# Condition products of two hybrid blocks: from TensorE matmuls to multiply-adds on VectorE in lots of four

## The chip, the cores and the metric

The kernel runs on one core of one Trainium2 chip. The metric is the time of one execution in microseconds (us) of device time; a version's time is the median of its runs. A profiled execution gives the span of its instructions and their trace. The engines are called TensorE (PE in the rows; PEld is its weight load), VectorE (DVE), ScalarE (ACT), GpSimd (POOL) and SyncE (SP). ACTq and SPq are the rows of instructions that issue DMAs.

## The reference

A block of two layers (dilated attention, then a state space layer) is followed by a block of two hybrid layers. All is float32, 1024 tokens by 1024 channels. What matters here is the modulation of the hybrid layers: two condition vectors (one for the tokens, one for the context) are multiplied with `w_mod`, which gives shift, scale and gate.

```python
c_act = jax.nn.silu(c)            # (1, 1024)
cc_act = jax.nn.silu(c_ctx)       # (1024,)
for l in range(2):
    x, xc = hybrid_layer(x, xc, c_act, cc_act, w_mod[l], b_mod[l], ...)

def hybrid_layer(...):            # w_mod[l]: (1024, 3072)
    shift, scale, gate = jnp.split(c_act @ w_mod + b_mod, 3, axis=-1)
    h = x * (1 + scale[:, None]) + shift[:, None]
    mod_c = jnp.split(cc_act @ w_mod[:, :n_mod * D_MODEL] + b_mod[:n_mod * D_MODEL], n_mod)
    hc = xc * (1 + mod_c[1]) + mod_c[0]
    ...
```

So there are two vectors of 1024 by two matrices of 1024x3072. The kernel does this work far ahead of the hybrid layers, while the attention layer runs, and keeps the results in DRAM (`mod_rows`).

## The kernel before

**The attention stage.** It walks over eight pairs of heads (hp 0 to 7) and, in each, over three segments (si 0 to 2), one for each group of the dilated attention. A segment has four unit pairs (p = 4*si to 4*si+3). For each, TensorE computes `scores`, VectorE adds the bias and takes the row minimum (`logits`, line 3747), ScalarE takes exponentials (`probs`), TensorE transposes them (`turn_p`), ScalarE copies them out of PSUM (`take_pt`), TensorE multiplies by v (`outputs`, lines 3003 and 3010, and at p % 4 == 3 a transposition of the statistics, line 3015), and VectorE evacuates (`evacuate`, lines 3762 to 3771). Between these steps TensorE computes the projections of the next pair of heads in three passes of split float32 (`proj`, line 2936): 24 matmuls of 512 columns for each half of 512 tokens. `seg_at` says how many are done ahead of each step. The order on every engine is written out by hand, and the engines meet in semaphores. A segment's last `outputs` comes at the start of the next segment, behind 12 projection matmuls.

The last segment (hp 7, si 2) has no projections. A projection half needs its PSUM bank free, that is the evacuation of the half two before it by ScalarE (`evac`, line 1226); behind every second half ScalarE rounds a slot of weights (line 3265) and GpSimd computes its rest (line 2766; for the next stage's weights lines 2757 and 2760).

**The merge.** In a pair's first segment VectorE also merges the three groups of the pair before (`merge_all`). The group weights go out to DRAM (`put_weights`, ScalarE at i == 2) and come back spread over 64 partitions (`spread_weights`, four loads of ScalarE's queue at i == 3, lines 3315 and 3318). VectorE waits for them at i == 4 (part 1, line 3815) and goes on at i == 5 (parts 2 and 0, lines 3818 and 3820). Here i runs from 0 to 7 in `segment_act` and `segment_dve`, two steps to a unit pair: at an even i come `logits` of the next pair and `evacuate` of the one before.

**The condition products.** The 2 x 3072 columns are cut into 12 visits of 512 columns, n = 3*(hp-4)+si, one in each segment of the head pairs 4 to 7. ScalarE loads the weights of visit n in the segment before, at i == 5, in two halves of 256 columns (1 MB each, line 1252). In segment n TensorE computes 12 projection matmuls, the last `outputs` of the segment before, eight more projection matmuls, waits for VectorE's evacuation and then does `mod_mul` (line 1268): 8 blocks of 128 rows by 4 blocks of 128 columns, each with a stationary operand of 32 columns, of which two hold the conditions and 30 are zero (`c_wide`). The four column blocks write four different groups of 32 PSUM partitions. VectorE adds the bias in `mod_add` (line 1278), and TensorE waits for that at the segment's first `outputs`.

Of the kernel before, what the change touches and what calls it, by code (L numbers as in the profile page):

```python
# [16 lines left out]
ALU = mybir.AluOpType  # L17
# [4 lines left out]
P = 128  # L22
# [115 lines left out]
def build(nc, io, out):  # L138
    x_in = io["x"].rearrange("b s d -> (b s) d")
    ctx = ExitStack()  # L140
    with ctx:
# [1092 lines left out]
        c_wide = region(29712, KT, 32)  # L1234
# [4 lines left out]
        m_wide, m_c, m_mul, m_sum, m_stored = [sem(n) for n in ("m_wide", "m_c", "m_mul", "m_sum", "m_stored")]  # L1239
# [7 lines left out]
        def load_mod_w(act, n):  # L1247
# [3 lines left out]
            for i in range(2):  # L1251
                act.dma_start(MOD_W[i], w[:, :, c0 + CTX * i:c0 + CTX * (i + 1)]).then_inc(m_w, 16)
# [8 lines left out]

        def mod_mul(pe, n):

            pe.wait_ge(m_wide, 2)
            pe.wait_ge(m_w, 32 * (n + 1))
            for k in range(KT):
                for c in range(4):
                    ins = nc.tensor.matmul(psum[32 * c:32 * c + 32, 6, 0:P], c_wide[:, k, :],
                                           MOD_W[c // 2][:, k, P * (c % 2):P * (c % 2) + P],
                                           start=(k == 0), stop=(k == KT - 1))  # L1270
            ins.then_inc(m_mul, 1)

        def mod_add(dve, n):
# [4 lines left out]
            nc.vector.tensor_tensor(MOD_ROWS[:, n], MOD_ROWS[:, n], psum[:, 6, 0:P], ALU.add).then_inc(m_sum, 1)  # L1278
# [1631 lines left out]
        def _(pe):  # L2910
# [78 lines left out]
            def outputs(hp, p):  # L2989
# [7 lines left out]
                if p % 4 == 0 and mod_of(hp, si) is not None:  # L2997
                    pe.wait_ge(m_sum, mod_of(hp, si) + 1)
# [50 lines left out]
            def segment(hp, si, par, prev, with_proj):  # L3049
# [175 lines left out]
        def _(act):  # L3225
# [168 lines left out]
            def segment_act(hp, si, par, prev, with_proj, more):  # L3394
# [17 lines left out]
                for i in range(8):  # L3412
# [196 lines left out]
        def _(dve):  # L3609
# [141 lines left out]
            def evacuate(hp, p, par):  # L3751
# [3 lines left out]
                if p % 4 == 3:  # L3755
# [6 lines left out]
                    nc.vector.tensor_copy(dst, src).then_inc(st_rows, 1)  # L3762
# [253 lines left out]
```

## Time and profile before

| | us |
|---|---|
| median of 3 runs (lowest to highest) | 3149.55 (3145.45 to 3152.84) |
| profiled execution, its own time | 3148.35 |
| its span, first to last instruction | 3146.5 |
| TensorE busy | 3056.2 (97%) |
| VectorE busy | 1497.5 (48%) |
| ScalarE busy | 1229.6 (39%) |
| GpSimd busy | 808.1 (26%) |

The busy time of an engine is the time in which at least one of its instructions runs; TensorE's matmuls overlap, so the mean of one (0.39 us for 512 columns) is longer than its pitch (0.23 us). The share is a mean over stages. The mean granted clock of TensorE is 0.993 of full speed. Times in the rows are counted from the start of the span. In a timeline each row gives the start, the duration, engine, line, operation and operands, how many such instructions are merged into it, and in brackets how long the engine had been idle and what ended it.

### The profile page before, as it was taken

To read this page: it belongs to the slowest core of one execution; us is meant where nothing else is said; L and a number is where in the kernel's file an instruction comes from. 1 tells how busy PE (TensorE), PEld (TensorE's weight loads), DVE (VectorE), ACT (ScalarE), POOL (GpSimd) and SP (SyncE) were. 2 spreads that over 40 slices of the span, in tenths; PEclk is the share of its full clock that TensorE was granted. 3 is DMA by queue.
4 is the path that set the end of the run, shared out by engine and by line. 5 is a ranking of instruction groups with operands and counts; after the bars stand their busy time and mean duration, and the time that the engine had idled before them with its cause. 6 is when DMAs were issued, how large, how long until landed. Compare 5 with 4: busy or idle time off the path is not lost.

```text
span 3146.5 us, 54425 instructions
## 1 busy us (share of the span) xinstructions
PE 3056.2 (97%) x22219; PEld 2474.9 (79%) x22219; DVE 1497.5 (48%) x3462; ACT 1229.6 (39%) x2590; POOL 808.1 (26%) x407
## 2 busy tenths in 40 slices
PE   7999999999999998999999999999999999999999
PEld 5877778788787786777888888877788788877777
DVE  3343232332313235659632535665556845565676
ACT  4443434444433434513321523345333333344342
POOL 2155565111112114133254111110223111111231
PEclk9999999999999999999999999999999999999999
DMA  6113223144423333423454311111003332111113
GB/s 198 46 49 88 74 74 88 54 130 119 121 92 91 98 86 103 138 71 107 146 189 144 109 41 41 39 28 32 25 28 112 114 79 54 33 34 33 36 47 141
DMA packets 327792, 262.22 MB, mean 83 GB/s; under 512 B 78123, under 2 KB 291659, under 8 KB 327548
## 3 DMA queue, kind: packets, MB, share of 16 engines
q1 hardware_dynamic: 187692, 131.09, 14.5%
q10 hardware_dynamic: 139856, 127.69, 13.6%
q8 instruction: 176, 2.88, 0.4%
q14 instruction: 68, 0.56, 0.1%
HBM read 215.50 MB, written 45.97 MB: 83 GB/s over the span
## 4 chain that ended last, share of the span: by engine, by line
PE 51%; DVE 5%; ACT 3%; issue 2%; DMA 1%; ACTq 0%; POOL 0%; DVEq 0%; POOLq 0%
PE psum L1550 24%; PE psum L387 10%; PE psum L312 5%; PE psum L1686 2%; PE psum L1666 2%; PE psum L1675 1%; DVE act_lo L2582 1%; PE psum L1590 1%; PE psum L1579 1%; PE psum L3177 1%; PE psum L1596 1%; PE psum L3186 0%; PE psum L3157 0%; PE psum L1623 0%; DVE arena L2344 0%
## 5 line engine op out<-in xcount | busy, mean ns | idle before, releaser
L2766 POOL TENSOR_TENSOR w_lo<-w_raw,w_hi 128x1024 fp32r<-128x1024 f32 x122 | 300.7, 2465 | 1434.8 <-ACT w_hi L3265 743.4
L1550 PE MATMUL psum<-act_hi,w_hi 128*128 128x512 f32 (+1 forms) x1376 | 513.5, 373 | 12.0 <-ACT arena L1779 6.3
L2936 PE MATMUL psum<-act_hi,w_hi 128*128 128x512 f32 x1280 | 505.1, 395 | 6.3 <-ACT arena L1226 5.4
L2936 PE MATMUL psum<-act_lo,w_hi 128*128 128x512 f32 x1280 | 507.4, 396 | 0.0
L2936 PE MATMUL psum<-act_hi,w_lo 128*128 128x512 f32 x1280 | 505.1, 395 | 0.0
L1550 PE MATMUL psum<-act_lo,w_hi 128*128 128x512 f32 (+1 forms) x1376 | 504.5, 367 | 0.0
L1550 PE MATMUL psum<-act_hi,w_lo 128*128 128x512 f32 (+1 forms) x1376 | 503.9, 366 | 0.0
L3747 DVE CUSTOM_DVE_ANT_0 arena<-psum,arena 128x256 f32<-128x256 f32 (+2 forms) x384 | 103.4, 325 | 445.5 <-PE psum L2985 178.0
L1550 PEld LDWEIGHTS psum<-act_hi,w_hi 128*128 128x128 f32 x1376 | 260.4, 189 | 68.4 <-issue 17.9
L1550 PEld LDWEIGHTS psum<-act_hi,w_lo 128*128 128x128 f32 x1376 | 260.7, 189 | 45.6 <-issue 5.5
L1550 PEld LDWEIGHTS psum<-act_lo,w_hi 128*128 128x128 f32 x1376 | 260.9, 190 | 43.9 <-issue 7.6
L2936 PEld LDWEIGHTS psum<-act_hi,w_hi 128*128 128x128 f32 x1280 | 241.6, 189 | 60.1 <-ACT arena L1226 6.4
L2936 PEld LDWEIGHTS psum<-act_lo,w_hi 128*128 128x128 f32 x1280 | 241.0, 188 | 58.9 <-issue 9.8
L2936 PEld LDWEIGHTS psum<-act_hi,w_lo 128*128 128x128 f32 x1280 | 240.7, 188 | 56.9 <-issue 8.3
L2757 POOL TENSOR_TENSOR w_hi<-w_raw,one 128x1024 fp32r<-128x1024 f32 x48 | 96.7, 2014 | 657.5 <-PE psum L1550 274.6
L1226 ACT ACTIVATE arena<-psum 128x512 f32<-128x512 f32 x144 | 133.3, 926 | 188.7 <-PE psum L2936 151.9
L3274 ACT ACTIVATE arena<-arena 128x256 f32<-128x256 f32 (+2 forms) x384 | 161.6, 423 | 73.3 <-DVE arena L3747 73.0
L1779 ACT ACTIVATE arena<-psum 128x512 f32<-128x512 f32 (+1 forms) x102 | 70.7, 694 | 200.3 <-PE psum L1550 197.5
L3329 ACT COPY arena<-psum 128x1024 f32<-128x1024 f32 x64 | 64.9, 1015 | 173.0 <-PE psum L3010 145.7
L2760 POOL TENSOR_TENSOR w_lo<-w_raw,w_hi 128x1024 fp32r<-128x1024 f32 x48 | 124.0, 2584 | 3.8
L1875 ACT COPY arena<-psum 128x640 f32<-128x640 f32 (+1 forms) x108 | 71.3, 660 | 128.6 <-PE psum L1686 97.9
L1866 ACT ACTIVATE arena<-arena 128x384 f32<-128x384 f32 (+1 forms) x96 | 56.8, 592 | 150.1 <-DVE arena L2106 150.1
(409 smaller groups left out, 5355.7 us busy)
## 6 DMA issues: line engine op xcount, KB each, us to landing
w_raw<-in_attn_w_in SPq DMA_DIRECT2D x80, 512.0 KB, 3.8
w_raw<-in_w_in SPq DMA_DIRECT2D x64, 512.0 KB, 3.9
spare<-in_w_mod ACTq DMA_DIRECT2D x24, 1024.0 KB, 8.4
x<-arena ACTq DMA_DIRECT2D x24, 512.0 KB, 2.9
arena<-weight_rows ACTq DMA_DIRECT2D x16, 512.0 KB
w_raw<-in_ssm_w_in SPq DMA_DIRECT2D x16, 512.0 KB, 3.7
arena<-mc_mat ACTq DMA_DIRECT2D x16, 512.0 KB, 4.1
arena<-x ACTq DMA_DIRECT2D x16, 512.0 KB, 5.4
```

Source lines behind the costliest of these rows:

```text
L312: ins = nc.tensor.matmul(psum[:, t, :], a[:, k, t * P:(t + 1) * P], w[:, par, i * 512:(i + 1) * 512], start=(k == 0 and a is act_hi and w ...
L387: ins = nc.tensor.matmul(psum[:, bank + c, :], a[:, k, t * P:(t + 1) * P], w[:, c * 512:(c + 1) * 512], start=(i == 0 and w is hi and a is ...
L1226: return nc.scalar.activation(dst, src, ACT.Copy, scale=SCALE if p % 3 == 0 else 1.0)
L1550: ins = nc.tensor.matmul(psum[:, n % 2, 0:c], w[:, slot % 2, k * P:(k + 1) * P], a[:, k, c0:c0 + c], start=(m == 0), stop=(m == 23))
L1779: C.activation(dst, src, ACT.Copy, scale=SCALE if (j < 3 and q == 0) or (j >= 3 and q == 1) else 1.0).then_inc(g_evac[n % 2], 1)
L1875: C.copy(PT2[h][:, c0:N_LOG], flat(6, 2)[:, c0:N_LOG]).then_inc(u_pt, 1)
L2757: G.tensor_tensor(w_hi[:, par], w_raw[:, par], one[:, 0:1].to_broadcast([P, 1024]), ALU.mult).then_inc(slot_hi, 1)
L2760: G.tensor_tensor(w_lo[:, par], w_raw[:, par], w_hi[:, par].bitcast(F32), ALU.subtract).then_inc(slot_split, 1)
L2766: G.tensor_tensor(w_lo[:, par], w_raw[:, par], w_hi[:, par].bitcast(F32), ALU.subtract).then_inc(slot_split, 1)
L2936: ins = nc.tensor.matmul(psum[:, h % 2, :], w[:, (3 + j) % 2, k * P:(k + 1) * P], a[:, k, c:c + 512], start=(m == 0), stop=(m == 23))
L3274: nc.scalar.activation(lg, lg, ACT.Exp, scale=-1.0, bias=st[:, 2 + h, u:u + 1], accum_out=st[:, h, u:u + 1]).then_inc(u_probs, 1)
L3747: nc.vector.tensor_tensor_reduce(LOG[:, a, logit_cols(g, u, h)], logit_psum(g, u, a, h), BIAS[:, h, bias_cols(g, u)], -1.0, 3e38, ALU.add, ...
```

## The change

The products move to VectorE. For each block of 128 rows (k) and each condition (i), one operation multiplies a 128x256 tile of weights with a scalar for each partition (the condition's value for that row) and adds it to a sum `MOD_SUM` of 128 partitions. A half of 256 columns takes 16 operations, a visit 32. They are done in lots of four, one after each step i of the segment before (`next_mod`), lots 0 to 3 for the first half of the columns, 4 to 7 for the second; visit 0 is done in four lots of eight at i = 4 to 7. TensorE then only adds up the 128 partitions: `mod_mul` has 8 matmuls in place of 32, with a stationary operand that has a column of ones, and stands at the start of the segment's last `outputs`. It waits for all 32 operations. `mod_add` follows inside `evacuate`.

The loads are issued by halves: the second half of a visit at i == 2 (behind lot 0), the first half of the visit after it at i == 5 (behind lot 4); for visit 0 both at i == 3. The eight projection matmuls that stood ahead of the product, its wait for the evacuation and the wait of `outputs` for `mod_add` go.

```diff
+        def mod_part(dve, n, half, k0, k1):
+            dve.wait_ge(m_w, 32 * n + (32 if n == 0 else 16 * (half + 1)))
+            if n == 0 and k0 == 0:
+                dve.wait_ge(m_c, 33)
+                dve.wait_ge(k_put, CHUNK_PUT * N_CHUNKS)
+            if n > 0:
+                dve.wait_ge(m_mul, n)
+            for k in range(k0, k1):
+                for i in range(2):
+                    w, total = MOD_W[half][:, k, :], MOD_SUM[:, i, CTX * half:CTX * half + CTX]
+                    c = c_cols[:, k, i:i + 1]
+                    if k == 0:
+                        nc.vector.tensor_scalar(total, w, c, None, ALU.mult).then_inc(m_part, 1)
+                    else:
+                        dve.wait_ge(m_part, 32 * n + 16 * half + 2 * k + i - 1)
+                        nc.vector.scalar_tensor_tensor(total, w, c, total, ALU.mult, ALU.add).then_inc(m_part, 1)
         def mod_mul(pe, n):
-            pe.wait_ge(m_wide, 2)
-            pe.wait_ge(m_w, 32 * (n + 1))
-            for k in range(KT):
+            if n == 0:
+                pe.wait_ge(n_pad, 3)
+            pe.wait_ge(m_part, 32 * (n + 1))
+            if n > 0:
+                pe.wait_ge(m_sum, n)
+            for i in range(2):
                 for c in range(4):
-                    ins = nc.tensor.matmul(psum[32 * c:32 * c + 32, 6, 0:P], c_wide[:, k, :],
-                                           MOD_W[c // 2][:, k, P * (c % 2):P * (c % 2) + P],
-                                           start=(k == 0), stop=(k == KT - 1))
+                    ins = nc.tensor.matmul(psum[32 * c:32 * c + 32, 6, 384:512], MOD_ONE[:, i, :],
+                                           MOD_SUM[:, i, P * c:P * c + P], start=(i == 0), stop=(i == 1))
             ins.then_inc(m_mul, 1)
@@ outputs
-                if p % 4 == 0 and mod_of(hp, si) is not None:
-                    pe.wait_ge(m_sum, mod_of(hp, si) + 1)
+                if p % 4 == 3 and next_mod(hp, si) is not None:
+                    mod_mul(pe, next_mod(hp, si))
@@ segment
-                if mod_of(hp, si) is not None:
-                    if with_proj:
-                        proj(hp, h0, at, at + 8)
-                        at += 8
-                    pe.wait_ge(u_evac, NU * hp + 8 * si)
-                    mod_mul(pe, mod_of(hp, si))
@@ segment_act
-                    if i == 5 and -1 <= m < N_MOD - 1:
-                        if m >= 0:
-                            act.wait_ge(m_mul, m + 1)
-                        load_mod_w(act, m + 1)
+                    if i == 2 and 0 <= m < N_MOD - 1:
+                        act.wait_ge(m_part, 32 * (m + 1) + 4)
+                        load_mod_w(act, m + 1, 1)
+                    if i == (7 if m == -1 else 5) and -1 <= m < N_MOD - 2:
+                        act.wait_ge(m_part, 32 * (m + 1) + 20)
+                        load_mod_w(act, m + 2, 0)
                     if i == 3 and m == -1:
                         act.wait_ge(k_put, CHUNK_PUT * N_CHUNKS)
                         act.wait_ge(k_cst, 32 * N_CHUNKS)
+                        for half in range(2):
+                            load_mod_w(act, 0, half)
                         load_mod_bias(act)
@@ evacuate, between the copy of the statistics and that of the outputs
+                    if next_mod(hp, p // 4) is not None:
+                        mod_add(dve, next_mod(hp, p // 4))
@@ segment_dve, after the merge parts of step i
+                    if next_mod(hp, si) == 0 and i >= 4:
+                        mod_part(dve, 0, i // 6, 4 * (i % 2), 4 * (i % 2) + 4)
+                    if next_mod(hp, si) is not None and next_mod(hp, si) > 0:
+                        mod_part(dve, next_mod(hp, si), i // 4, 2 * (i % 4), 2 * (i % 4) + 2)
```

## Rows read from the trace of the kernel before

**Rows 1.** Busy time of each engine in the stretch of the products.

```profile
core 0: us, PE busy (x) PEld busy (x) DVE busy (x) ACT busy (x) POOL busy (x), PEclk, DMA share, GB/s
655.00:1197.00 542.00, 538.72 (x4625) 430.86 (x4618) 144.02 (x571) 216.41 (x524) 97.12 (x41) 1.00 0.36 105
```

**Rows 2.** Groups of instructions, shapes apart; busy us, mean ns, idle before.

```profile
L1268 PE MATMUL psum<-spare,arena 128*32 128x128 f32 x768 | 23.5, 274 | 1.2 <-DVE arena L3771 1.2
```

**Rows 3.** Timeline of TensorE around the first product.

```profile
662.13 0.39 PE L2936 MATMUL psum<-act_lo,w_hi 128*128 128x512 f32 x1
662.45 1.95 PE L1268 MATMUL psum<-spare,arena 128*32 128x128 f32 x64
664.33 1.09 PE L2967 MATMUL psum<-ident,arena 128*128 128x128 f32 x8
```

**Rows 4.** Groups of VectorE at the end of the kernel, shapes apart.

```profile
L2505 DVE SCALAR_TENSOR_TENSOR arena<-arena 128x512 f32<-128x512 f32 x2 | 1.4, 750 | 0.0
```

**Rows 5.** Timeline of VectorE, the same two operations.

```profile
3142.61 1.42 DVE L2505 SCALAR_TENSOR_TENSOR arena<-arena 128x512 f32<-128x512 f32 x2
```

**Rows 6.** Timeline, TensorE and VectorE at the end of segment 4/1.

```profile
752.22 0.89 PE L3010 MATMUL psum<-arena 64*64 64x128 f32 x24
756.93 0.89 PE L3010 MATMUL psum<-arena 64*64 64x128 f32 x24
...
753.71 0.42 DVE L3771 TENSOR_TENSOR arena<-arena,psum 128x256 f32<-128x256 f32 x1
```

**Rows 7.** Timeline, VectorE and TensorE at the end of segment 4/0.

```profile
693.76 1.99 DVE L3815 TENSOR_TENSOR arena<-arena 128x1024 f32<-128x1024 f32 x1 [4.16 <-DMA arena<-weight_rows]
...
698.81 0.47 DVE L3767 COPY arena<-psum 128x256 f32<-128x256 f32 x1
...
700.64 0.46 PE L3003 MATMUL psum<-arena 64*64 64x64 f32 x16
```

**Rows 8.** The same places at the end of segment 7/0.

```profile
1132.85 2.00 DVE L3815 TENSOR_TENSOR arena<-arena 128x1024 f32<-128x1024 f32 x1 [5.20 <-DMA arena<-weight_rows]
...
1138.68 0.46 PE L3003 MATMUL psum<-arena 64*64 64x64 f32 x16
```

**Rows 9.** Timeline at the end of segment 3/2: VectorE, GpSimd, TensorE.

```profile
656.11 0.42 DVE L3771 TENSOR_TENSOR arena<-arena,psum 128x256 f32<-128x256 f32 x1
...
658.69 2.38 POOL L2766 TENSOR_TENSOR w_lo<-w_raw,w_hi 128x1024 fp32r<-128x1024 f32 x1 [13.68 <-ACT w_hi L3265]
...
659.30 1.10 PE L3010 MATMUL psum<-arena 64*64 64x128 f32 x32
```

**Rows 10.** Timeline of segment 6/0: GpSimd and VectorE.

```profile
985.07 4.81 POOL L2766 TENSOR_TENSOR w_lo<-w_raw,w_hi 128x1024 fp32r<-128x1024 f32 x1 [14.29 <-ACT w_hi L3265]
...
987.53 4.23 DVE L3820 TENSOR_TENSOR arena<-arena 128x1024 f32<-128x1024 f32 x1
```

**Rows 11.** Timeline of ScalarE's queue in segment 4/0.

```profile
684.11 0.58 ACTq L3315 DMA_DIRECT2D arena<-weight_rows  x1
```

**Rows 12.** Stretch after 694 us: columns as in Rows 1.

```profile
694.00:699.00 5.00, 5.00 (x38) 3.94 (x38) 5.00 (x4) 1.36 (x3) 0.00 (x0) 1.00 1.10 375
```

**Rows 13.** Timeline at the end of segment 5/1: GpSimd, TensorE.

```profile
901.15 2.39 POOL L2766 TENSOR_TENSOR w_lo<-w_raw,w_hi 128x1024 fp32r<-128x1024 f32 x1 [12.54 <-ACT w_hi L3265]
...
902.18 0.89 PE L3010 MATMUL psum<-arena 64*64 64x128 f32 x24
```

**Rows 14.** Timeline at the start of segment 7/2: TensorE, GpSimd.

```profile
1192.36 0.89 PE L3010 MATMUL psum<-arena 64*64 64x128 f32 x24
...
1196.64 1.09 PE L2967 MATMUL psum<-ident,arena 128*128 128x128 f32 x8
...
1192.44 1.90 POOL L2757 TENSOR_TENSOR w_hi<-w_raw,one 128x1024 fp32r<-128x1024 f32 x1 [10.54 <-PE psum L2936]
1194.41 2.39 POOL L2760 TENSOR_TENSOR w_lo<-w_raw,w_hi 128x1024 fp32r<-128x1024 f32 x1
```

**Rows 15.** Stretches around a pause of TensorE in a hybrid layer.

```profile
2204.00:2206.00 2.00, 0.17 (x1) 0.17 (x2) 1.50 (x7) 2.00 (x8) 0.00 (x0) 0.96 0.00 0
2206.00:2208.00 2.00, 2.00 (x25) 1.67 (x29) 0.88 (x3) 0.33 (x2) 0.00 (x0) 0.50 0.21 25
```

More of the change, by code:

```diff
@@ L1231, in build @@
         halves = lambda g2: slice(64 * g2, 64 * g2 + 64)
-        c_wide = region(29712, KT, 32)
+        MOD_SUM = region(29168, 2, 512)
+        MOD_ONE = region(26128, 2, 32)
         N_MOD = 12
@@ L1238, in build @@
         mod_rows = dram("mod_rows", (2, 2, 3072))
-        m_wide, m_c, m_mul, m_sum, m_stored = [sem(n) for n in ("m_wide", "m_c", "m_mul", "m_sum", "m_stored")]
+        m_part, m_c, m_mul, m_sum, m_stored = [sem(n) for n in ("m_part", "m_c", "m_mul", "m_sum", "m_stored")]
         m_bias, m_w = sem("m_bias"), sem("m_w")
@@ L1245, in mod_of, with next_mod, load_mod_w @@
             return n if 0 <= n < N_MOD else None
-        def load_mod_w(act, n):
+        def next_mod(hp, si):
+            n = 3 * (hp - 4) + si + 1
+            return n if 0 <= n < N_MOD else None
+        def load_mod_w(act, n, half):
             l, c0 = n // 6, 512 * (n % 6)
             w = io["w_mod_2"][l].rearrange("(k p) c -> p k c", p=P)
-            for i in range(2):
-                act.dma_start(MOD_W[i], w[:, :, c0 + CTX * i:c0 + CTX * (i + 1)]).then_inc(m_w, 16)
+            act.dma_start(MOD_W[half], w[:, :, c0 + CTX * half:c0 + CTX * (half + 1)]).then_inc(m_w, 16)
         def load_mod_bias(act):
@@ L1277, in mod_add @@
             dve.wait_ge(m_mul, n + 1)
-            nc.vector.tensor_tensor(MOD_ROWS[:, n], MOD_ROWS[:, n], psum[:, 6, 0:P], ALU.add).then_inc(m_sum, 1)
+            nc.vector.tensor_tensor(MOD_ROWS[:, n], MOD_ROWS[:, n], psum[:, 6, 384:512], ALU.add).then_inc(m_sum, 1)
         def store_mod(act, l):
@@ L3852, in segment_dve @@
                     merge_all(hp - 1, 1 - par, "three")
-                if mod_of(hp, si) is not None:
-                    mod_add(dve, mod_of(hp, si))
                 dve.wait_ge(v_turned, 6 * hp + (2 * si + 2))
@@ L3880, in segment_dve @@
                         nc.vector.memset(PAD[0:31, :, :], 0.0).then_inc(n_pad, 1)
-                        nc.vector.memset(c_wide[:, :, :], 0.0).then_inc(m_wide, 1)
-                        dve.wait_ge(m_wide, 1)
-                        nc.vector.tensor_copy(c_wide[:, :, 0:2], c_cols[:, :, :]).then_inc(m_wide, 1)
+                        nc.vector.memset(MOD_ONE[:, :, :], 0.0).then_inc(n_pad, 1)
+                        dve.wait_ge(n_pad, 2)
+                        nc.vector.memset(MOD_ONE.rearrange("p a b -> p (a b)")[:, 0:64:33], 1.0).then_inc(n_pad, 1)
                     if hp == 0 and si == 2 and i < 4:
                         k_squares(1 << i)
+                    if next_mod(hp, si) == 0 and i >= 4:
+                        mod_part(dve, 0, i // 6, 4 * (i % 2), 4 * (i % 2) + 4)
+                    if next_mod(hp, si) is not None and next_mod(hp, si) > 0:
+                        mod_part(dve, next_mod(hp, si), i // 4, 2 * (i % 4), 2 * (i % 4) + 2)
                     if si == 1 and i == 4:
```

## The prediction

> **What bounds the kernel now.** I began with the busy times of each engine over the stretch in which the condition products run, from 655 to 1197 us [rows 1]. The reader is to see TensorE (PE) busy for 538.7 of 542 us at the full clock, VectorE (DVE) for only 144 us. So here TensorE sets the time: what it is spared is won, and a wait that it gets is lost, microsecond for microsecond. VectorE has 398 us to spare, but it works in order, and what counts is what it has between two waits of TensorE. So I then read the timeline at the places where the new waits stand: the end of each of the three segments of a head pair, where `outputs` of the segment's last unit pair now begins with `mod_mul`.
>
> **What is removed from TensorE.** The 384 products (two records each) have 23.5 us busy [rows 2]. One visit: the last projection matmul before it starts at 662.13, its slot is 0.23, and the next work starts at 664.33 [rows 3], so a product costs 664.33 - 662.36 = 1.97 us. Eight matmuls of the same form in place of 32 cost 8/32 of 1.88 = 0.47. The gain is 1.50 us for each visit; the last visit stands in a segment with no projections and is counted by itself below, so 11 x 1.50 = **-16.5 us**. The eight projection matmuls that stood ahead of the product are not lost or saved: they move behind the scores, and everything after that in the segment moves with them by 1.8 us.
>
> **What is added to VectorE.** 12 x 32 operations of 128x256, nearly all scalar_tensor_tensor with a scalar per partition. Rows have this form at 128x512: 750 ns each [rows 4], two in a row in 1.42 us [rows 5], so the second starts 0.67 after the first, which is 512 elements at 0.96 per ns (0.533) plus 0.137. For 256 that gives 0.267 + 0.137 = 0.40 us. A lot of four is 1.6 us, 12 x 8 lots are 155 us. The waits inside a lot are on the operation two before, ended by then. In the middle of a segment this is hidden behind the projections: the unit pairs there are 8 to 12 us apart and a pair brings some 2.3 us of VectorE work plus two lots, 3.2. It costs 0 there; without that cover it would be the whole 3.2.
>
> **Where it is not hidden.** `mod_mul` waits for lot 7, and lots 6 and 7 come after the evacuation of the third unit pair. In a middle segment TensorE starts these outputs at 752.22 and comes to the last outputs at 756.93; the second evacuating operation starts at 753.71 [rows 6], leaves VectorE free 0.34 later, and eight operations plus 0.13 for the end and the release give 753.71 + 0.34 + 3.23 + 0.13 = 757.41. That is 0.5 us late. The third segments come to the same 0.5. For the six such ends (products 2, 3, 5, 6, 8, 9): 3.0 us.
>
> In the first segment of a pair VectorE merges the groups of the pair before. It waits for the weight rows until 693.76, and the evacuation starts at 698.81 only; TensorE is at the last outputs at 700.64 [rows 7]. Now lots 4 to 7 all stand in that chain, since lot 4 is behind the merge that waits: 693.76 + 5.05 + 4 x 1.62 + 0.35 + 0.13 = 705.8, so 5.1 us late. The last such pair has less room, 1132.85 to 1138.68 [rows 8], and 6.3 us by the same sum; the other two give 5.8 and 5.2 (the one at 984 us has a merge of 4.23 in its chain already [rows 10]). Together 22.4 us. ScalarE stands in this too: its load at i == 5 waits for lot 4, so it evacuates a projection half some 7 us later than now, and TensorE stands still for that instead, inside the same lateness. I count it once.
>
> Product 0 is done in lots of eight at i = 4 to 7: from 656.11 + 0.34, 16 x 0.404 + 0.13 gives 663.0 against 659.30 [rows 9], 3.7 us.
>
> **The half load that is moved.** ScalarE issued both halves at i == 5, behind the four loads of the weight rows (i == 3, first at 684.11 [rows 11]). Now one half of 1 MB goes out at i == 2, ahead of them in the same queue. When only these loads are served they move 375 GB/s [rows 12], so 1 MB takes 2.8 us; the queue is idle for some of it (24 KB are written and waited for meanwhile). Bounds 0 and 2.8; I take 1.0, since the issue comes some 1.5 us before 684.11. Four times: 4 us. The other half is issued after lot 4 with most of a segment to land: 0. The bias loads and SP's loads keep their places; one half is issued behind lot 0, so nothing of SP's queue waits for it.
>
> **GpSimd.** At 985.07 GpSimd's split took 4.81 us instead of 2.39, and VectorE's merge at 987.53 took 4.23 where its like took 2.2 [rows 10]: two operations that read SBUF stand in each other's way, and the one that comes second waits for the whole of the other. The lots read two operands from SBUF. A split of 2.4 us starts 1.0 us before the last outputs [rows 13] in five of the six ends above, so inside lots 6 and 7; at 658.69 [rows 9] it lies inside product 0's. In a first segment it lies inside the lengthened chain. The bounds are 0 and 2.4 for each. At 985 the split had let two merges pass before it got its turn, so where only one microsecond of lots is left I take half, 5 x 1.2 = 6.0; where the chain is long, all: 4 x 2.4 = 9.6, and 2.4 for product 0.
> The Trainium skill (SBUF — State Buffer, "SBUF: two separate sides") says that VectorE with two SBUF inputs and GpSimd take one port pair as an exclusive lock for a whole instruction. By that rule each of the five would pay the full 2.4, and the sum below would be 6 us more; the trace shows the lock, but also the split passed over.
>
> **The last visit.** Segment 3 of the last pair has no projections. TensorE is at the last outputs at 1192.36 and at the transposes of v at 1196.64; GpSimd splits at 1192.44 and 1194.41 [rows 14]. The lots start near 1192.1: one operation, the first split, one operation, the second split (to 1197.2), then six in 2.4 us, so 1199.75. Product 0.47, outputs and statistics 1.1: the transposes start at 1201.3, **+4.7 us**, its gain included.
>
> **The clock.** After TensorE had stood idle for 1.8 us at 2204, the granted clock went from full to half for some 3.4 us [rows 15]; matmuls run half as fast there, 1.7 us lost. I charge 1.7 to each wait over 1.9 us: four first segments, product 0, and half of the five: 7.5 x 1.7 = 12.8 us. Bounds: 0, and 2.5 each.
>
> **Sum.** Waits 22.4 + 3.0 + 3.7 = 29.1; loads 4.0; GpSimd 9.6 + 6.0 + 2.4 = 18.0; last visit 4.7; clock 12.8: 68.6. Less 16.5: **+52 us**. The profiled execution took 3148.35, so 3200.5; the median is 1.2 above it: **3202 us**.
>
> **Rivals.** (a) *Such short operations do not meet the splits*, and the short waits do not move the clock. Then the waits are 29.1, the last visit +0.6, gain 16.5: +13, 3163 us. For it: the split passed over at 985. Against: every long pair that met. (b) *Every meeting of a lot with a split costs its whole 2.4 us*, with the load at 2.8 and the clock at its upper bound: +52 + 6 + 7 + 9 = +74, 3224 us. For it: the merge of 4.23. Against: in the short ends only two or three operations are left when the split comes. (That case is the rule of the Trainium skill, SBUF — State Buffer, named above.) (c) *The lots are hidden.* If an operation took 0.27 us or less (twice the rate on the elements), lots 6 and 7 would end before TensorE arrives, and the first segments would have to free 5 us by weight rows that come earlier. Then it is faster by up to 12 x 1.5 = 18 us, 3132 us. It decides once all waits together stay below 16.5 us. Against it: no operation with two SBUF inputs in the rows runs faster than one element per cycle. (d) *Waits and gain cancel*: two first-segment waits of 5 us and a few short ones, 3150 us.
>
> **Chances.** The forecast 0.50, (a) 0.20, (b) 0.13, (c) 0.10, (d) 0.07. This kernel's measurement can tell about 0.2%, 6.3 us, from no change. Range 3156 to 3226: below lies (c), (d), and above little of (b). The likeliest case's own range is 3180 to 3220. Faster 0.10, same 0.07, slower 0.83.
>
> **What the profile would show.** TensorE's busy time for the product a quarter, some 6 us. An idle time ahead of the product ended by VectorE's lots: 0.5 to 3 us at the ends of middle and third segments, 6 to 9 us at first segments, part of it ahead of a projection half, ended by ScalarE's evacuation. VectorE's busy time up by some 170 us; the longest of the new operations near 2.8 us where a split lies under it, the split itself hardly longer. The weight rows' merge starts about 1 us later after the scores of the second unit pair. Clock dips after the waits of the first segments. I am wrong if the operation's pitch is not 0.40 us, if lots 4 and 5 run before the merge's wait ends, or if TensorE reaches the last outputs later than now for another reason, which would make room for the lots.

## The result and the profile after

The changed kernel takes 3212.56 us (median of 4 runs, 3208.60 to 3215.35) against 3149.01 for the kernel before in the same comparison: ratio 1.0201, 95% interval 1.0188 to 1.0213. It is slower, far outside the noise; whether by more or by less than 2% the interval leaves open. The profiled execution took 3208.6 with a span of 3206.8, so 60.3 us more than before's 3146.5. Mean granted clock 0.984 against 0.993.

The same work that lay between 655 and 1197 us [rows 1] now ends near 1258, so the first row is to be laid beside that of before. The second shows the stretch of equal length.

```profile
core 0: us, PE busy (x) PEld busy (x) DVE busy (x) ACT busy (x) POOL busy (x), PEclk, DMA share, GB/s
655.00:1258.00 603.00, 544.40 (x4049) 432.95 (x4047) 311.05 (x949) 215.86 (x525) 103.84 (x42) 0.95 0.33 95
...
655.00:1197.00 542.00, 491.85 (x3668) 391.00 (x3667) 280.81 (x859) 195.48 (x477) 86.98 (x34) 0.95 0.35 99
```

TensorE idles for 603 - 544.4 = 58.6 us, where it idled for 3.3. That is 55 of the 60 us. Its busy time went up by 5.7 although the products got shorter, and the granted clock of the stretch fell from 1.00 to 0.95. Who ended the idle time stands in the waits of TensorE, between 655 and 1260 us (us in total, times, longest):

```profile
PE psum L1294 <- DVE arena L1283: 41.0, 12, 7.0
PE psum L2961 <- ACT arena L1226: 16.2, 4, 5.9
PE psum L2981 <- DVE arena L3770: 1.4, 1, 1.4
```

L1294 is the product and L1283 the new operation. L2961 is a projection (before: L2936) that needs ScalarE's evacuation L1226; that one had in turn waited for a load issue whose semaphore the lots raise. The groups of the whole trace, shapes apart:

```profile
L1283 DVE SCALAR_TENSOR_TENSOR arena<-spare,c_cols,arena 128x256 f32<-128x256 f32 x336 | 167.8, 568 | 0.0
...
L3840 DVE TENSOR_TENSOR arena<-arena 128x1024 f32<-128x1024 f32 x8 | 18.4, 2298 | 50.0 <-DMA arena<-weight_rows 50.0
L1280 DVE TENSOR_SCALAR arena<-spare,c_cols 128x256 f32<-128x256 f32 x48 | 16.5, 387 | 0.9 <-DVE arena L3865 0.9
...
L1294 PE MATMUL psum<-arena 128*32 128x128 f32 x192 | 10.8, 359 | 41.0 <-DVE arena L1283 41.0
```

The products have 10.8 us busy where [rows 2] had 23.5, over half of it at half clock.

**A first segment.** The timeline of segment 4/0, to be laid beside [rows 7] and [rows 11]:

```profile
682.85 0.60 ACTq L3327 DMA_DIRECT2D weight_rows<-arena  x1
...
683.90 0.40 ACTq L1257 DMA_DIRECT2D spare<-in_w_mod  x1
684.10 3.24 DVE L1283 SCALAR_TENSOR_TENSOR arena<-spare,c_cols,arena 128x256 f32<-128x256 f32 x8
...
687.11 0.59 ACTq L3334 DMA_DIRECT2D arena<-weight_rows  x1
...
699.64 1.98 DVE L3840 TENSOR_TENSOR arena<-arena 128x1024 f32<-128x1024 f32 x1 [7.80 <-DMA arena<-weight_rows]
...
703.42 1.06 ACT L1226 ACTIVATE arena<-psum 128x512 f32<-128x512 f32 x1 [10.17 <-DVE arena L1283]
...
704.54 0.79 PE L2961 MATMUL psum<-act_hi,w_hi 128*128 128x512 f32 x1 [4.32 <-ACT arena L1226]
...
706.65 3.18 POOL L2791 TENSOR_TENSOR w_lo<-w_raw,w_hi 128x1024 fp32r<-128x1024 f32 x1 [12.51 <-ACT w_hi L3284]
...
707.82 5.07 DVE L1283 SCALAR_TENSOR_TENSOR arena<-spare,c_cols,arena 128x256 f32<-128x256 f32 x8
713.15 1.08 PE L1294 MATMUL psum<-arena 128*32 128x128 f32 x16 [3.43 <-DVE arena L1283]
```

Eight operations run in 3.24 us at 684.10. At 707.82 eight of them take 5.07, with GpSimd's split (L2791) under the first; the split too is longer than its usual 2.39. The half load goes out 1.05 us after the weights' way to DRAM, ahead of the spread load, and the merge (L3840) starts 12.5 us after that spread load is issued, where it was 9.65 (684.11 to 693.76 in [rows 7, 11]). TensorE stands still twice: 4.32 us for ScalarE ahead of 704.54 and 3.43 ahead of the product.

**A short end and the last one.** The end of segment 4/2, and below it the start of segment 7/2 (the product of the last visit), to be laid beside [rows 13, 14]:

```profile
814.65 5.34 DVE L1283 SCALAR_TENSOR_TENSOR arena<-spare,c_cols,arena 128x256 f32<-128x256 f32 x8
...
816.92 2.39 POOL L2791 TENSOR_TENSOR w_lo<-w_raw,w_hi 128x1024 fp32r<-128x1024 f32 x1 [13.71 <-ACT w_hi L3284]
...
820.25 0.64 PE L1294 MATMUL psum<-arena 128*32 128x128 f32 x16 [2.67 <-DVE arena L1283]
820.82 1.10 PE L3035 MATMUL psum<-arena 64*64 64x128 f32 x32
...
1244.12 6.99 DVE L1283 SCALAR_TENSOR_TENSOR arena<-spare,c_cols,arena 128x256 f32<-128x256 f32 x8
...
1244.47 1.89 POOL L2782 TENSOR_TENSOR w_hi<-w_raw,one 128x1024 fp32r<-128x1024 f32 x1 [10.55 <-PE psum L2961]
...
1246.45 2.40 POOL L2785 TENSOR_TENSOR w_lo<-w_raw,w_hi 128x1024 fp32r<-128x1024 f32 x1
1251.36 1.08 PE L1294 MATMUL psum<-arena 128*32 128x128 f32 x16 [7.04 <-DVE arena L1283]
```

Eight operations undisturbed take 3.24 us, as at 684.10; the eight at 814.65 took 5.34, longer by 2.1, and those at 1244.12 took 6.99, longer by 3.8 under two splits of 4.3 together. The product itself, 820.25 to 820.82, takes 0.57 us. The six ends of middle and third segments, called short ends here, waited 0.55 (the one with no split in reach) and five times 2.66 or 2.67.

### The profile page after: what moved, and what is told of

Read it like the earlier page. It is cut to its first block, busy times and chain, and to the rows that moved or that the text cites. A ratio compares the mean times of both kernels' runs of the same rounds, so it can differ in the third digit from the quotient of the medians.

```text
span 3206.8 us, 53749 instructions
## 1 busy us (share of the span) xinstructions
PE 3063.7 (96%) x21643; PEld 2478.9 (77%) x21643; DVE 1665.3 (52%) x3846; ACT 1228.9 (38%) x2590; POOL 808.6 (25%) x407
## 3 DMA queue, kind: packets, MB, share of 16 engines
q1 hardware_dynamic: 187692, 131.09, 14.2%
## 4 chain that ended last, share of the span: by engine, by line
PE 49%; DVE 5%; ACT 3%; issue 2%; DMA 1%; ACTq 1%; POOL 0%; DVEq 0%; POOLq 0%
PE psum L1575 24%; PE psum L387 9%; PE psum L312 5%; PE psum L1711 2%; PE psum L1691 2%; PE psum L1700 1%; DVE act_lo L2607 1%; PE psum L1615 1%; PE psum L1604 1%; PE psum L3196 1%; PE psum L3205 0%; PE psum L1621 0%; PE psum L3176 0%; PE psum L428 0%; PE psum L1648 0%
## 5 line engine op out<-in xcount | busy, mean ns | idle before, releaser
L2791 POOL TENSOR_TENSOR w_lo<-w_raw,w_hi 128x1024 fp32r<-128x1024 f32 x122 | 303.9, 2491 | 1486.0 <-ACT w_hi L3284 792.0
L2961 PE MATMUL psum<-act_hi,w_hi 128*128 128x512 f32 x1280 | 509.1, 398 | 20.5 <-ACT arena L1226 19.6
L2961 PE MATMUL psum<-act_lo,w_hi 128*128 128x512 f32 x1280 | 510.4, 399 | 0.0
L2961 PE MATMUL psum<-act_hi,w_lo 128*128 128x512 f32 x1280 | 505.7, 395 | 0.0
L2961 PEld LDWEIGHTS psum<-act_hi,w_hi 128*128 128x128 f32 x1280 | 242.6, 190 | 80.3 <-ACT arena L1226 22.4
L1575 PEld LDWEIGHTS psum<-act_lo,w_hi 128*128 128x128 f32 x1376 | 260.7, 189 | 43.7 <-issue 7.5
L2961 PEld LDWEIGHTS psum<-act_lo,w_hi 128*128 128x128 f32 x1280 | 242.8, 190 | 58.9 <-issue 9.9
L2961 PEld LDWEIGHTS psum<-act_hi,w_lo 128*128 128x128 f32 x1280 | 242.6, 189 | 54.9 <-issue 5.6
L1226 ACT ACTIVATE arena<-psum 128x512 f32<-128x512 f32 x144 | 133.5, 927 | 223.2 <-PE psum L2961 148.7
L1283 DVE SCALAR_TENSOR_TENSOR arena<-spare,c_cols,arena 128x256 f32<-128x256 f32 x336 | 167.8, 568 | 0.0
L3348 ACT COPY arena<-psum 128x1024 f32<-128x1024 f32 x64 | 64.9, 1015 | 179.3 <-PE psum L3035 147.4
```

Of the source, the lines that this page charges most:

```text
L1226: return nc.scalar.activation(dst, src, ACT.Copy, scale=SCALE if p % 3 == 0 else 1.0)
L1283: nc.vector.scalar_tensor_tensor(total, w, c, total, ALU.mult, ALU.add).then_inc(m_part, 1)
L1575: ins = nc.tensor.matmul(psum[:, n % 2, 0:c], w[:, slot % 2, k * P:(k + 1) * P], a[:, k, c0:c0 + c], start=(m == 0), stop=(m == 23))
L2791: G.tensor_tensor(w_lo[:, par], w_raw[:, par], w_hi[:, par].bitcast(F32), ALU.subtract).then_inc(slot_split, 1)
L2961: ins = nc.tensor.matmul(psum[:, h % 2, :], w[:, (3 + j) % 2, k * P:(k + 1) * P], a[:, k, c:c + 512], start=(m == 0), stop=(m == 23))
```

## The experiments

The kernel before gave 3148 to 3149 us in every batch. Medians against it:

| kernel | median us (lowest to highest) | ratio to before, 95% interval |
|---|---|---|
| after | 3212.56 (3208.60 to 3215.35) | 1.0201 (1.0188 to 1.0213) |
| after, half load behind the spread | 3210.48 (3201.99 to 3212.07) | 1.0191 (1.0173 to 1.0208) |
| after, short splits | 3177.64 (3174.98 to 3184.46) | 1.0092 (1.0075 to 1.0109) |
| after, narrow | 3168.84 (3160.53 to 3172.68) | 1.0071 (1.0054 to 1.0088) |
| before, half load early | 3166.58 (3154.26 to 3174.99) | 1.0060 (1.0041 to 1.0078) |
| before, short splits | 3148.76 (3144.01 to 3153.87) | 1.0002 (0.9993 to 1.0011) |
| lots early | 3144.47 (3138.79 to 3149.74) | 0.9984 (0.9973 to 0.9995) |
| all lots early | 3142.88 (3136.61 to 3147.85) | 0.9982 (0.9973 to 0.9990) |
| after, loads early | 3201.47 (3200.11 to 3204.54) | 1.0173 (1.0159 to 1.0187) |
| after, narrow, loads early | 3161.16 (3153.67 to 3165.74) | 1.0040 (1.0026 to 1.0054) |
| all lots early, short splits | 3136.00 (3129.82 to 3140.42) | 0.9959 (0.9944 to 0.9973) |
| after, narrow, loads early, short splits | 3138.91 (3134.18 to 3145.09) | 0.9973 (0.9963 to 0.9983) |
| after, loads early, short splits | 3176.32 (3170.76 to 3178.01) | 1.0088 (1.0075 to 1.0101) |

**1. The half load behind the spread.** The kernel after with one number changed:

```diff
-                    if i == 2 and 0 <= m < N_MOD - 1:
+                    if i == 3 and 0 <= m < N_MOD - 1:
```

> The changed kernel, with the half load of a visit issued at i == 3, behind the four loads of the weight rows, not at i == 2 ahead of them. All else as changed. Theory (the load ahead of the weight rows makes VectorE's merge late, and four lots stand behind that merge): the merge's wait ends some 3.5 us earlier after the second unit pair's outputs in each of four first segments, TensorE's waits there fall by as much, with the clock 3195 to 3200 us against 3212.6. Rival (the weight rows are late for another reason, or the lateness is absorbed): 3212 within 3 us.

Measured 3210.48, not told apart from after: a miss for the theory, inside the rival's range. The merges did start earlier in the segment, 13.4 to 17.3 us after the weights went out in place of 15.8 to 18.4, 8.8 us in all. But the second half of the columns then landed behind the weight rows, and lot 4, which needs it, stands next in VectorE's order:

```profile
DVE arena L1280 <- DMA spare<-in_w_mod: 3.4, 4, 1.5
```

So 3.4 of the 8.8 us went to a new wait. TensorE's waits at the products were 42.7 us (41.0 in after), those for ScalarE 12.3 (16.2). Where the rest of the 8.8 us went is not shown.

**2. Short splits.** The kernel after, GpSimd's `split_lo` in the last four head pairs cut (the low parts of the weights are left out there for 960 of 1024 columns):

```diff
-            def split_lo(m, par):
+            def split_lo(m, par, n=1024):
...
-                G.tensor_tensor(w_lo[:, par], w_raw[:, par], w_hi[:, par].bitcast(F32),
+                G.tensor_tensor(w_lo[:, par, 0:n], w_raw[:, par, 0:n], w_hi[:, par, 0:n].bitcast(F32),
...
-                split_lo(m, par)
+                split_lo(m, par, 64)
```

> The changed kernel, with GpSimd's split of the attention weights in head pairs 4 to 7 done on 64 of 1024 columns (the rest of the low part of these weights is left as it was, so part of the computation is left out). Theory (a lot that meets a split waits for its whole 2.4 us): TensorE's wait ahead of the product falls from 2.8 to 0.5 us in five of the six middle and third segments, by 2.4 us in first segments and for product 0, little for the last visit, whose splits are of another line; with the clock some 30 us: about 3182 us. Rival (the lots are late by their own length alone): no change, 3212 us.

Measured 3177.64, 35 us less. The same end as above, segment 4/2, in the timeline of this kernel (seven of the lot's last eight operations):

```profile
812.36 2.92 DVE L1283 SCALAR_TENSOR_TENSOR arena<-spare,c_cols,arena 128x256 f32<-128x256 f32 x7
...
814.63 0.37 POOL L2791 TENSOR_TENSOR w_lo<-w_raw,w_hi 128x64 fp32r<-128x64 f32 x1 [15.75 <-ACT w_hi L3284]
```

The product behind it, at 815.93, waited 0.64 where it had waited 2.67. So a split under a lot costs TensorE 2.03 us in each of these five ends, and the waits of TensorE in the two chief groups read

```profile
PE psum L1294 <- DVE arena L1283: 23.4, 12, 7.0
PE psum L2961 <- ACT arena L1226: 13.8, 5, 6.1
```

which is 20.0 us less than after's 41.0 and 16.2. Up to the last product, the stretches at half clock fell from 64.9 to 41.0 us. This trace doesn't account for all of the 35 us, for its execution took 3184.46, the slowest of the four. From the first product to the last it is 26.0 us shorter than after's: 20.0 are the waits, the other 6 busy time of TensorE, of which less is at half clock.

**3. Before with short splits,** the same edit in the kernel before, as a control.

> The kernel before with the same short splits of GpSimd in head pairs 4 to 7 (part of the low part of the weights is left out). Control for the short splits of the changed kernel. Theory: no one waits for these splits there: 3149 us within 3 us. Rival (the splits themselves hold TensorE or the loads): faster by over 6 us, and then that much of the other run's gain isn't the lots'.

Measured 3148.76, ratio 1.0002. GpSimd's splits cost the kernel before nothing that can be measured; the 35 us come only where lots and splits are together.

**4. Narrow operations.** The kernel after, each product operation on 16 of its 256 columns (the condition products are not computed in full; one operation more, not shown, sets the sums to zero first):

```diff
                     c = c_cols[:, k, i:i + 1]
+                    w, total = w[:, 0:16], total[:, 0:16]
```

> The changed kernel, with each of VectorE's 384 operations on 16 of its 256 columns (the other columns of the sums stay zero: most of the products is left out). Loads, waits, order and the new product on TensorE are as changed. Theory (the length of the lots is what TensorE waits for): the waits ahead of the product are gone but for some tenths, the gain of 16.5 us comes out: 3130 to 3138 us, faster than before. Rival (the place of the product, its waits and the moved loads cost by themselves): over 3149 us.

Measured 3168.84, a miss for the theory; the rival asked for over 3149. It is 43.7 us less than after, but still 21 above the kernel before. The length of the operations was not the whole cost.

**5. Before with the half load early.** Products on TensorE as before, only the loads moved, one half to i == 2 ahead of the spread (visit 0's loads stay at i == 5, not shown):

```diff
-                    if i == 5 and -1 <= m < N_MOD - 1:
-                        if m >= 0:
-                            act.wait_ge(m_mul, m + 1)
-                        load_mod_w(act, m + 1)
+                    if i == 2 and 0 <= m < N_MOD - 1:
+                        act.wait_ge(m_mul, m + 1)
+                        load_mod_w(act, m + 1, 1)
+                    if i == 5 and 0 <= m < N_MOD - 1:
+                        load_mod_w(act, m + 1, 0)
```

> The kernel before, with its loads split: one half of the next visit's weights at i == 2, ahead of the weight rows, the other at i == 5. The product stays on TensorE. Theory: the weight rows come 2 to 4 us later, but only 1.3 us or so of room is missing behind them, since no lots stand there: 3149 to 3158 us. Rival (the moved load is itself a main cost of the change): over 3165 us.

Measured 3166.58: a miss for the theory again, and in the rival's range. The edit priced at 4 us in the prediction costs 18.6 in the kernel before by itself (by the interval 13 to 25). Its timeline in segment 5/0 shows how:

```profile
844.49 2.01 DVE L3818 TENSOR_TENSOR arena<-arena 128x1024 f32<-128x1024 f32 x1 [7.52 <-DMA arena<-weight_rows]
...
847.45 2.39 POOL L2765 TENSOR_TENSOR w_lo<-w_raw,w_hi 128x1024 fp32r<-128x1024 f32 x1 [9.74 <-ACT w_hi L3264]
847.53 4.06 DVE L3823 TENSOR_TENSOR arena<-arena 128x1024 f32<-128x1024 f32 x1
...
851.99 0.46 PE L3002 MATMUL psum<-arena 64*64 64x64 f32 x16 [3.92 <-DVE arena L3770]
```

The merge starts 16.5 us after the weights went out, where it was 13.7, so 2.9 us late. Its last part now lies where GpSimd splits, takes 4.06 in place of 2.2, and the evacuation behind it comes 3.92 us late for TensorE. Three such waits are 9.7 us; the trace of before has none. The profiled execution of this kernel lies 6 us below its median, so the trace accounts for a part.

**6. Loads early.** The kernel after, lots where the change put them; the second half load goes out at unit 0, ahead of everything:

```diff
-                    if i == 2 and 0 <= m < N_MOD - 1:
-                        act.wait_ge(m_part, 32 * (m + 1) + 4)
+                    if i == 0 and 0 <= m < N_MOD - 1:
+                        act.wait_ge(m_part, 32 * (m + 1) + 1)
                         load_mod_w(act, m + 1, 1)
...
-                        act.wait_ge(m_part, 32 * (m + 1) + 20)
+                        act.wait_ge(m_part, 32 * (m + 1) + 17)
```

> The kernel after, its lots where the change put them; only the half loads are issued earlier: the second half at unit 0 instead of 2, so that it no longer stands ahead of the weight rows and their spread load in ScalarE's DMA queue (the first half stays at unit 5). If the load is worth by itself what it cost in the kernel before (about 18 us), this gives 3190 to 3200 and VectorE's merge starts again about 13.5 to 14 us after the put. If it is worth more, because the late merge and the lots push each other, 3175 to 3190. Rival: the lots of the second half, and GpSimd's split among them, are what counts in the kernel after, and the load is covered by them: 3205 to 3213.

Measured 3201.47, 11 us less, 1.5 above the range of the load theory and below the rival's. In three of the four first segments the merges are back at 13.4 to 13.8 us after the weights went out (13.2 to 14.2 in before); in 5/0 it is still 16.7. TensorE's waits:

```profile
PE psum L1294 <- DVE arena L1283: 50.2, 12, 7.0
PE psum L2961 <- ACT arena L1226: 5.5, 3, 3.2
```

The wait ahead of the projection fell by 10.7 us and the wait at the product rose by 9.2: the product of a first segment waits for the end of VectorE's chain, and what TensorE doesn't lose on the way there it loses at the product. Both together fell by 1.5 us only. From the first product to the last the trace is 7.9 us shorter (581.9 against 589.8), so most of that is clock: 51.2 us at half in place of 64.9.

**7. Narrow operations with the loads early** (the condition products are not computed in full).

> The kernel after with both the narrow operations (16 of 256 columns in each product operation, so that the condition products are not computed in full) and the half load issued at unit 0. If the narrow run was held back by the late half load alone, this leaves only what TensorE is saved: 12 visits of about 1.4 us at full clock, some of it lost to the small lots: 3130 to 3138. Rival: what held the narrow run back is the order of the work on VectorE or TensorE (the sum read by TensorE inside the visit, the wait for the evacuation), not the load: 3155 to 3169.

Measured 3161.16: a miss for the theory, in the rival's range. But the trace shows another cause than the rival's order of work, namely the splits. Of the last lots in segment 4/0 the timeline says

```profile
698.27 2.77 DVE L1284 SCALAR_TENSOR_TENSOR arena<-spare,c_cols,arena 128x16 f32<-128x16 f32 x4
698.47 2.40 POOL L2792 TENSOR_TENSOR w_lo<-w_raw,w_hi 128x1024 fp32r<-128x1024 f32 x1 [8.73 <-ACT w_hi L3285]
...
701.31 1.31 DVE L1284 SCALAR_TENSOR_TENSOR arena<-spare,c_cols,arena 128x16 f32<-128x16 f32 x8
...
702.88 1.08 PE L1295 MATMUL psum<-arena 128*32 128x128 f32 x16 [3.53 <-DVE arena L1284]
```

Eight operations of 16 columns take 1.31 us, but four of them with a split under them 2.77. Even such short ones pay for most of a split.

**8. The same with short splits** (the condition products are not computed in full, nor the low parts of the weights).

> The kernel after with 16 of 256 columns in each product operation (the condition products are not computed in full), the half load issued at unit 0, and GpSimd's split cut to 64 of 1024 columns in the last four head pairs. In the narrow run with the earlier load the last lot of four visits still met a 2.40 us split of GpSimd (one operation of the lot took 2.39 us instead of 0.23), and TensorE waited 16.8 us in five products. If that meeting is what keeps the narrow runs from the gain on TensorE, its 12 visits of 1.4 us are left here: 3130 to 3138. Rival: the visit's new order on VectorE and TensorE costs by itself: 3150 to 3160, with waits at the products that no split explains.

Measured 3138.91, 0.9 above the theory's range and far from the rival's. The waits at the products are down to 7.7 us, and the kernel is 9.2 us faster than before: that is about what the change spares TensorE (16.8), less the waits that are left.

**9. Full operations, loads early, short splits** (the low parts of the weights are not computed in full).

> The kernel after with its full operations where the change put them, the half load at unit 0 and the short splits of GpSimd. The short splits alone gave back 35 us and the load alone 11. If the two are separate costs, they add: 3163 to 3170, and what is left above the kernel before is the time of the lots themselves at the end of each visit. Rival: both give back the same waits, since the products wait for whichever comes last: 3172 to 3178.

Measured 3176.32, the rival's figure: the two savings don't add. With the splits short, the early load gives 1.3 us, without it 11.1. Product waits 30.3 us.

**10. The lots early.** For visits 1 to 11 the lots stand at i = 0 to 4, as 4, 4, 8, 8 and 8 operations, the last eight ahead of the merge, so that VectorE does them while it waits for the weight rows; loads early as in 6, not shown again.

```diff
-                    if next_mod(hp, si) is not None and next_mod(hp, si) > 0:
-                        mod_part(dve, next_mod(hp, si), i // 4, 2 * (i % 4), 2 * (i % 4) + 2)
+                    if (next_mod(hp, si) or 0) > 0 and i < 4:
+                        mod_part(dve, next_mod(hp, si), i // 3, (0, 2, 4, 0)[i], (2, 4, 8, 4)[i])
...
+                    if (next_mod(hp, si) or 0) > 0 and i == 4:
+                        mod_part(dve, next_mod(hp, si), 1, 4, 8)
                     if si == 0 and prev and i in MERGES:
```

> The changed kernel, with all 32 operations of visits 1 to 11 at i = 0 to 4 (4, 4, 8, 8, 8), the last eight ahead of the merge that waits for the weight rows, and the half loads at i == 0 and i == 5. Visit 0 is as changed. Theory (it is the place of the lots, not their amount): the products 1 to 10 find their sums ready; waits are left for product 0 (3.5 us) and perhaps the last: 3138 to 3146 us, faster than before by some 0.2%. Rival (VectorE's load itself, or its meetings with GpSimd, holds the logits up wherever the lots stand): over 3155 us.

Measured 3144.47, as the theory said, 68 us less than after and 0.16% less than before. The last eight now lie in the merge's wait, though a split lies under them (4.83 us for eight):

```profile
691.19 2.40 POOL L2791 TENSOR_TENSOR w_lo<-w_raw,w_hi 128x1024 fp32r<-128x1024 f32 x1 [8.43 <-ACT w_hi L3284]
...
691.81 4.83 DVE L1283 SCALAR_TENSOR_TENSOR arena<-spare,c_cols,arena 128x256 f32<-128x256 f32 x8
696.56 1.98 DVE L3840 TENSOR_TENSOR arena<-arena 128x1024 f32<-128x1024 f32 x1
```

**11. Visit 0 early too,** in lots of eight at i = 2 to 5, its loads at i == 0 and the first load of visit 1 at i == 5.

> As the one before, and visit 0 in lots of eight at i = 2 to 5, its loads at i == 0. Theory: product 0's wait goes too, 4 to 6 us with the clock: 3132 to 3142 us. Rival (early loads of visit 0 collide with other work of the segment): no faster than the one before.

Measured 3142.88, 0.9 above the expected range: 1.6 us less than experiment 10, which these intervals don't tell apart, though product 0's wait of 3.4 us is gone from the trace. It is 0.18% less than before, interval 0.9973 to 0.9990. This is the best version that computes everything, and it beats both kernels. What it still loses lies in segment 5/0: a merge of 4.05 us under a split of 2.98, and a product that waits 4.46.

**12. The same with short splits** (the low parts of the weights are not computed in full).

> The version with all lots early and the half loads early, and GpSimd's split cut to 64 of 1024 columns in the last four head pairs (the rest of the low parts is not computed there). If what VectorE and GpSimd still make each other wait is what remains of the cost, 3132 to 3139. Rival: the remaining loss is in DMA order and in ScalarE's evacuations, GpSimd has nothing to do with it: 3140 to 3145.

Measured 3136.00, 6.9 us less: the theory that the splits are most of what remains holds. The product in 5/0 waits 0.41 us in place of 4.46.

## Why the prediction was right, point by point

The forecast was 3202 us and slower; it came to 3212.6. Step by step, in us, the measured column from the profiled execution:

| step | predicted | measured |
|---|---|---|
| product at full clock | 1.97 to 0.47 | 1.97 to 0.57 |
| pitch of an operation | 0.404 | 0.396 (684.10: 3.24 for 8, with its end) |
| TensorE's waits in four first segments | 22.4 + 9.6 + 4.0 = 36.0 | 32.9 (16.2 + 16.7) |
| in six short ends | 3.0 + 6.0 = 9.0 | 13.9 |
| product 0 | 3.7 + 2.4 = 6.1 | 3.4 |
| wait in the last visit | 7.4 (1192.36 to 1199.75) | 7.0 |
| all waits | 58.5 | 57.2 |
| clock | 12.8 | some 22 |

**Right.** The sign, the places and the chief mechanism. VectorE, in order, had 398 us to spare and still came late at each of the twelve products, for the lots sat behind the evacuation or the waiting merge. Experiments 10 and 11 prove it from the other side: the same 384 operations of the same width, placed ahead of the waits, cost nothing, and 68 to 70 us come back (the early load is in this, worth 11 by itself). In experiment 11 VectorE is busy for 293.96 of the 537 us between 655 and 1192, a larger share than after's 311.05 of 603. The wait for ScalarE ahead of a projection half, inside the lateness of a first segment, came as foreseen, and so did the wait of the last visit. VectorE's busy time rose by 167.8 us, where 170 had been foreseen.

**Luck.** That all waits together came within 1.3 us of the forecast is luck: the first segments came out 3.1 us below, the short ends 4.9 above, product 0 2.7 below. By the difference of experiment 2, the splits cost 9.9 us in the four first segments (9.6 predicted), 10.1 in the short ends (6.0) and nothing at product 0 (2.4). A slip of the working touches no figure above: rival (b) puts the clock's upper bound at 9 us more, but 2.5 in place of 1.7 gives 6 for its 7.5 waits.

**Short ends mis-sized.** The prediction took half a split, 1.2 us, for each of five ends, "where only one microsecond of lots is left". All five paid nearly the whole: a wait of 2.66 or 2.67 us with a split, 0.63 or 0.64 with a short one. By the rule of the Trainium skill (SBUF — State Buffer, "SBUF: two separate sides") that the prediction set against its row, each would pay in full, and here the trace agrees, with 2.03 us of 2.39. The row of 985.07 that had argued for a half shows a split that let two merges pass; under the lot at 816.92 it let none pass, but took its turn behind the operation that was running. And the prediction's 1.0 us from the split to the last outputs [rows 13] is that of segment 5/1; in the third segments of before it is 0.6 (803.94 to 804.56 in 4/2).

**Product 0 mis-sized the other way.** There the split paid, and with short splits TensorE waited the same 3.37 us:

```profile
655.84 5.63 DVE L1283 SCALAR_TENSOR_TENSOR arena<-spare,c_cols,arena 128x256 f32<-128x256 f32 x14
...
659.22 4.46 POOL L2791 TENSOR_TENSOR w_lo<-w_raw,w_hi 128x1024 fp32r<-128x1024 f32 x1 [13.50 <-ACT w_hi L3284]
661.61 1.08 PE L1294 MATMUL psum<-arena 128*32 128x128 f32 x16 [3.37 <-DVE arena L1283]
```

Fourteen operations in 5.63 us are 0.40 each, none lengthened, and the split took 4.46 and ended 2.2 us behind them. Who pays, the lot or the split, the runs show both ways; what decides it they don't show.

**The moved load mis-sized.** The prediction had 1.0 us each between bounds of 0 and 2.8. Counted from where the weights went out, the merges started 3.6, 4.7, 2.4 and 2.0 us later, 12.8 in all. Of this 9.4 lie between the issue of the first spread load and the merge (2.9, 1.7, 2.3 and 2.5 us, near the 2.8 that 1 MB takes), and 3.4 come from a later issue of the spread load. Still the sum of the first segments came out lower than predicted; that matmuls at half clock behind the first wait take up part of the lateness, so that less is left to wait for, is argued and not tested. In the kernel after the load is worth 11.1 us (experiment 6), in the kernel before 18.6 (experiment 5), where its timeline shows it pushing the merge into a split.

**The clock mis-sized.** This is the term that makes up the difference. TensorE's idle time is up by 55.3; its busy time by 5.7, though twelve products are 1.40 shorter, 16.8 together. So 22.5 us of busy time are from the lower clock. The granted clock of the trace has twelve stretches at half up to the last product, of 3.4 or 6.8 us, 64.9 together (before, in this work: none). Four windows of after (PEclk is the third number from the end):

```profile
661.00:664.00 3.00, 2.39 (x44) 2.03 (x48) 0.47 (x2) 0.00 (x0) 2.68 (x1) 0.57 0.28 97
702.00:706.00 4.00, 1.46 (x4) 1.17 (x5) 4.00 (x6) 2.58 (x4) 0.00 (x0) 0.55 0.43 133
713.00:716.00 3.00, 2.85 (x38) 2.38 (x39) 0.69 (x3) 0.00 (x0) 0.00 (x0) 0.50 0.01 2
820.00:823.00 3.00, 2.75 (x59) 2.25 (x60) 0.78 (x3) 0.34 (x1) 0.00 (x0) 1.00 0.60 175
```

The prediction counted one stretch of 3.4 us for each first segment. Each has two waits, for ScalarE and for the product, and so two stretches, mostly of 6.8: 47.8 us at half clock in four segments. It charged nothing for the last visit, where 6.8 us ran at half from 1248.5 on. After 820 the clock stayed full behind a wait of 2.67. Since both ledgers have nearly the same waits, the clock's 9.7 us above its term are what the forecast was short of (61.0 us more in this stretch, 52 predicted).

**What two-by-two the runs give.** With full operations: 3212.6, loads early 3201.5, short splits 3177.6, both 3176.3. Narrow: 3168.8, loads early 3161.2, both 3138.9. So taking the split away gives 35, 25 or 22 us, the load 11, 8 or 1, narrowing from 256 to 16 columns 44, 40 or 37. They are not separate costs that add to one number, but three ways to make one chain on VectorE end later, and one that is gone uncovers or hides another. The prediction's GpSimd term of 18.0 is to be laid beside the 20.0 us of waits that short splits took away; of the other 15 the traces show 6, as busy time of TensorE, and the rest is more than these two single executions can tell. What stays open: in experiment 5 single runs spread over 21 us, where those of before spread over 7 to 18 in a batch. Behind one and the same wait, 2.67 us at the end of segment 4/2, the clock stayed full in after and fell to half in experiments 1 and 6; whether this makes the spread was not tested.

## What to carry to other kernels

An engine that is half idle can still be late at every meeting point: before work is given to it, look at what stands between its last wait and the next thing that the bound engine needs, and put the new work into the idle time ahead of a wait, not behind it. With the loads early in both, the same 384 operations cost 53 us behind the evacuation and the merge (experiment 6) and nothing ahead of them (experiment 11). When a transfer is moved, ask what waits for the one behind it in the same queue: 1 MB ahead of a small load that VectorE waits for cost 18.6 us in a kernel that was otherwise left alone. And price a new wait of TensorE with the clock: here 57 us of waits took another 22 in matmuls at half clock.

## What the runs showed of the hardware

- VectorE's product operations, with two inputs from SBUF, and GpSimd's split didn't run at once. Under a split of 2.39 us eight operations took 5.34 in place of 3.24, and four of only 16 columns took 2.77, where eight took 1.31. But at 659.22 the split waited out the lot (4.46 us) and the lot ran at 0.40 each. In [rows 10] it had let two merges pass; here it was some five operations of a lot. The copy out of PSUM at 707.49 ran under a split, in 0.46 us where it usually takes 0.41.
- The operation with a scalar per partition has a pitch of 0.396 us for 128x256 and 0.155 for 128x16 (1.31 us for 8, the last one 0.23), so by a straight line between the two some 0.14 of it doesn't depend on the columns.
- In after, TensorE's clock fell to half at each wait of 3.35 us or more at a product, at all four for ScalarE (one of them 2.29 us, ahead of 1016.46), and at two of the five of 2.66 to 2.67 (at 931.5 and 981.66, not at 820, 1092 and 1141), for 3.4 or 6.8 us. In experiments 1 and 6 it fell at the wait of 2.67 at the end of 4/2 too.
